# Softmax attention: a joined tile is turned before the preceding tile's value products, and three seams between stages are changed

## What is computed

```python
s = jnp.einsum('bhiqd,bhikd->bhiqk', q_blk, k).astype(jnp.float32) * scale
s = s + bias.transpose(0, 3, 1, 2)[:, :, None]
p = jax.nn.softmax(s, axis=-1)
a = p[:, :, 0] - lam * p[:, :, 1]
return jnp.einsum('bhqk,bhkv->bhqv', a, v.astype(jnp.float32))
...
o_b = rms_norm(o_b.transpose(0, 2, 1, 3), diff_norm_w[i]) * (1 - lambda_init)
...
mixed = jnp.concatenate([o_a, o_b], axis=-1) @ w_out[i]
x = x + g_a[:, None, :] * mixed
```

```python
ya = ya * jax.nn.sigmoid(ya @ glu_w.astype(jnp.float32) + glu_b.astype(jnp.float32))
yb = fnet_mix(ub, f_w)
y = jnp.concatenate([ya, yb], axis=-1).astype(z.dtype) * jax.nn.silu(z)
return y @ w_out
```

## Time and profile before

| | us |
|---|---|
| median of 3 runs (2230.5 to 2232.33) | 2231.55 |
| time of the profiled execution | 2230.68 |
| its span | 2228.9 |
| attention loop, from the first biased map to the last output taken | 393 to 545 |
| block of the product mix begins | 553 |
| block of the product u begins | 1388 |
| block of the product eo begins | 1766 |

### The profile page before, as it was taken

One profiled execution on the slowest core, in us unless ns is written; L12 is line 12 of the kernel. 1 busy time (PEld: TensorE's weight loads), 2 busy tenths in 40 slices (PEclk: granted clock), 3 DMA queues, 4 the chain that ended last, 5 costly groups with the idle time before them and its releaser, 6 DMA issues. The chain is left out here.

```text
span 2228.9 us, 29464 instructions
## 1 busy us (share of the span) xinstructions
PE 2133.6 (96%) x11276; PEld 1735.0 (78%) x11276; DVE 1565.2 (70%) x2299; ACT 812.2 (36%) x1130; POOL 941.4 (42%) x718
## 2 busy tenths in 40 slices
PE   6999999998999999999999999999997999999997
PEld 4887787787777888888777786888877787777876
DVE  5775516998768888888768776869985637764344
ACT  4104433777234333444323224114225323342331
POOL 0222344431425888888556455111000021798710
PEclk9999999999999999999999999999998999999998
DMA  7595733332332333333577764493458323111131
GB/s 276 210 331 167 207 125 115 110 119 76 144 114 84 115 130 131 131 113 103 210 250 265 237 206 171 159 299 120 142 175 304 124 73 119 48 48 49 56 132 76
DMA packets 155430, 337.74 MB, mean 152 GB/s; under 512 B 14038, under 2 KB 92790, under 8 KB 152184
## 3 DMA queue, kind: packets, MB, share of 16 engines
q1 hardware_dynamic: 152292, 330.75, 43.7%
q10 hardware_dynamic: 3000, 5.15, 0.7%
HBM read 259.52 MB, written 93.09 MB: 158 GB/s over the span
## 5 line engine op out<-in xcount | busy, mean ns | idle before, releaser
L282 POOL TENSOR_TENSOR w_lo<-w_staged,w_hi 128x1024 fp32r<-128x1024 f32 x26 | 64.6, 2487 | 355.1 <-ACT w_hi L232 355.0
L2342 POOL TENSOR_TENSOR w_lo<-w_staged,w_hi 128x1024 fp32r<-128x1024 f32 x31 | 80.3, 2591 | 252.3 <-ACT w_hi L2323 252.3
L232 ACT CAST w_hi<-w_staged 128x1024 fp32r<-128x1024 f32 (+1 forms) x33 | 33.8, 1023 | 216.0 <-DMA w_staged<-in_w_u 40.5
L3736 POOL TENSOR_TENSOR w_lo<-w_staged,w_hi 128x512 fp32r<-128x512 f32 x61 | 83.4, 1368 | 59.1 <-ACT w_hi L3732 59.1
L2323 ACT CAST w_hi<-w_staged 128x1024 fp32r<-128x1024 f32 x31 | 32.5, 1049 | 157.9 <-PE ps_in L2351 104.9
L2351 PE MATMUL ps_in<-h_hi,w_hi 128*128 128x512 f32 x272 | 86.9, 400 | 1.0 <-DVE h_lo L1918 1.0
L3732 ACT CAST w_hi<-ff_room 128x512 fp32r<-128x512 f32 x60 | 36.7, 612 | 134.7 <-POOL ff_room L3753 130.2
L2351 PE MATMUL ps_in<-h_lo,w_hi 128*128 128x512 f32 x272 | 85.1, 394 | 0.0
L3440 POOL TENSOR_TENSOR ff_room<-s_par 128x480 f32<-128x480 f32 x32 | 39.6, 1237 | 100.0 <-PE ps_n L3481 50.9
L468 POOL TENSOR_TENSOR w_lo<-w_staged,w_hi 128x512 fp32r<-128x512 f32 x40 | 64.5, 1617 | 22.7 <-ACT w_hi L464 22.5
L3112 PEld LDWEIGHTS ps_attentions<-x_in,att_aT 128*128 128x128 f32 x512 | 59.6, 191 | 13.2 <-issue 10.6
(11 more groups left out here) (822 smaller groups left out, 7026.6 us busy)
## 6 DMA issues: line engine op xcount, KB each, us to landing
w_staged<-in_w_ff SPq DMA_DIRECT2D x46, 512.0 KB, 3.6
x_in<-in_w_ada SPq DMA_DIRECT2D x16, 1024.0 KB, 7.6
scratch_bias<-scratch_line SPq DMA_DIRECT2D x32, 512.0 KB, 7.7
kst_tok<-scratch_bias SPq DMA_DIRECT2D x32, 512.0 KB, 3.3
ada_w<-in_w_ada SPq DMA_DIRECT2D x8, 2048.0 KB, 11.0
scratch_x<-x SPq DMA_DIRECT2D x3, 4096.0 KB, 15.0
scratch_ff_a<-mixed SPq DMA_DIRECT2D x22, 512.0 KB, 2.9
ff_raw<-scratch_ff_a SPq DMA_DIRECT2D x20, 512.0 KB, 4.8
```

Source lines behind the costliest of these rows:

```text
L232: nc.scalar.copy(st.hi[i % 2][:, 0:widths[i]], st.staged[i % 2][:, 0:widths[i]]).then_inc(st.hi_ready, 1)
L282: nc.gpsimd.tensor_tensor(st.lo[i % 2][:, 0:widths[i]], st.staged[i % 2][:, 0:widths[i]], st.hi[i % 2][:, 0:widths[i]].bitcast(F32), ALU.s ...
L2342: nc.gpsimd.tensor_tensor(st.lo[i % 2][:, :], st.staged[i % 2][:, :], st.hi[i % 2][:, :].bitcast(F32), ALU.subtract).then_inc(st.split, 1)
L3736: self.nc.gpsimd.tensor_tensor(self.slot(self.st.lo, q, m), self.weights[m], self.slot(self.st.hi, q, m).bitcast(F32), ALU.subtract).then_ ...
```

## The change

Four things are changed.

1. In the attention loop PE does `turn(n - 1)` before `multiply(n - 2)`, not behind it. DVE's program in the loop stays as it is.
2. The end of the attention: `scale(2)` stands before the last `take`, not behind it; the last head is scaled, turned and placed in two halves of four tiles; and DVE makes only one `f_lo` there, the second one being made at the head of the next block (`low_ready=1`).
3. In `project` the `keep_warm` products are issued before the parts' own waits and not behind them. This changes an order only in the product u (`warm=7`); in the last product, the only other one with `warm`, the parts have nothing to do on PE.
4. In the gate block (`glu`) ACT and DVE split the first two strips of `y` for the product eo already (`split_ahead` and the lines in `mix`), and eo's own `SplitParts` begins at the third strip (`ready=EO_READY`). The tiles `o_hi` and `o_lo` get a place in memory that is free that early.

```diff
@@ both_attentions, PE
             def turn_head(h):
-                pe.wait_ge(scaled, h + 1)
                 if h >= 2:
                     pe.wait_ge(placed, h - 1)
-                for t in range(TT):
-                    last = nc.tensor.transpose(ps_s[:, 2 * (h % 2) + t // 4, t % 4 * P:t % 4 * P + P], o[:, h * TT + t, :], ident)
-                last.then_inc(turned_back, 1)
+                for half in range(2):
+                    if h == HEADS - 1 or half == 0:
+                        pe.wait_ge(scaled, h + half + 1)
+                    for t in range(half * TT // 2, (half + 1) * TT // 2):
+                        last = nc.tensor.transpose(ps_s[:, 2 * (h % 2) + t // 4, t % 4 * P:t % 4 * P + P], o[:, h * TT + t, :], ident)
+                    if h == HEADS - 1 or half == 1:
+                        last.then_inc(turned_back, 1)
...
                     pe.wait_ge(biased, 2 * N)
                     turn_head(0)
+                if 1 <= n <= N:
+                    turn(n - 1)
                 if n >= 2:
                     multiply(n - 2)
-                if 1 <= n <= N:
-                    turn(n - 1)
@@ both_attentions, ACT
-            for h in range(2, HEADS):
+            for h in range(2, HEADS - 1):
                 place(h)
+            for first in range(0, TT, TT // 2):
+                place(HEADS - 1, first, TT // 2)
@@ both_attentions, DVE
                     add_bias(n)
+                if n == N + 2:
+                    scale(2)
                 if n >= 3:
                     take(n - 3)
...
-            scale(2)
             mean(1)
             factor(1)
-            scale(HEADS - 1)
-            for k in range(2):
-                dve.wait_ge(nm.hi_ready, split0 + k + 1)
-                nc.vector.tensor_tensor(f_lo[:, k, :], mixed[:, k, :], f_hi[:, k, :].bitcast(F32), ALU.subtract).then_inc(nm.split, 1)
+            for first in range(0, TT, TT // 2):
+                scale(HEADS - 1, first, TT // 2)
+            dve.wait_ge(nm.hi_ready, split0 + 1)
+            nc.vector.tensor_tensor(f_lo[:, 0, :], mixed[:, 0, :], f_hi[:, 0, :].bitcast(F32), ALU.subtract).then_inc(nm.split, 1)
@@ project, PE
+            keep_warm(nc, st.g, ps[0][:, 0:2 * P], warm)
             for b in before:
                 b.tensor(pe)
-            keep_warm(nc, st.g, ps[0][:, 0:2 * P], warm)
@@ the gate block
             def mix(dve, k):
-                nc.vector.tensor_tensor(y[:, k, :], x[:, k, :], sig[:, k, :], ALU.mult)
+                if k == EO_READY + 1:
+                    dve.wait_ge(tabled, 1)
+                multiplied = nc.vector.tensor_tensor(y[:, k, :], x[:, k, :], sig[:, k, :], ALU.mult)
+                if k == EO_READY + 1:
+                    multiplied.then_inc(tabled, 1)
+                    dve.wait_ge(tabled, 2)
+                    for r in range(EO_READY):
+                        dve.wait_ge(nm.hi_ready, eo_split0 + r + 1)
+                        nc.vector.tensor_tensor(eo_lo[:, r, :], y[:, r, :], eo_hi[:, r, :].bitcast(F32), ALU.subtract).then_inc(nm.split, 1)
...
+                def split_ahead(self, act):
+                    act.wait_ge(gated, EO_READY + 1)
+                    for r in range(EO_READY):
+                        nc.scalar.copy(eo_hi[:, r, :], y[:, r, :]).then_inc(nm.hi_ready, 1)
```

More of the change, by code:

```diff
@@ L261, in _ @@
             for i in range(n, n + 2):
+                if open_gate is not None and i == n:
+                    beside.split_ahead(act)
                 if stats is not None and i == n + 1:
@@ L1554, with __init__ @@
 class SplitParts(Part):
[L1557 removed]
+    def __init__(self, nc, nm, x, kb, hi, lo, open_gate=None, ready=0, low_ready=None):
         self.open_gate, self.ready = open_gate, ready
+        self.low_ready = ready if low_ready is None else low_ready
         self.nc, self.nm, self.x, self.kb, self.hi, self.lo = nc, nm, x, kb, hi, lo
@@ L1567, in scalar @@
             self.nc.scalar.copy(self.hi[:, k, :], self.x[:, k, :]).then_inc(self.nm.hi_ready, 1)
-            if k == 0 and behind_first is not None:
+            if k == self.ready and behind_first is not None:
                 behind_first()
-            if self.open_gate is not None and k == self.open_gate.BEHIND:
+            if self.open_gate is not None and k == self.ready + self.open_gate.BEHIND:
                 self.open_gate.scalar(act)
     def vector(self, dve, behind_first=None):
-        for k in range(self.ready, self.kb):
+        for k in range(self.low_ready, self.kb):
             dve.wait_ge(self.nm.hi_ready, self.split0 + k + 1)
@@ L3240, in factor, with scale @@
                 dve.wait_ge(factored, 5 * q + 5)
-            def scale(h):
-                rows = slice(h * TT, (h + 1) * TT)
+            def scale(h, first=0, tiles=TT):
+                rows = slice(h * TT + first, h * TT + first + tiles)
                 if h == 0 or h == HEADS - 1:
                     dve.wait_ge(taken, rows.stop)
-                nc.vector.tensor_tensor(o[:, rows, :], o[:, rows, :], fac[:, rows].unsqueeze(2).to_broadcast([P, TT, P]),
+                nc.vector.tensor_tensor(o[:, rows, :], o[:, rows, :], fac[:, rows].unsqueeze(2).to_broadcast([P, tiles, P]),
                                         ALU.mult).then_inc(scaled, 1)
@@ L5382, in build @@
         with ExitStack() as ctx:
-            split = SplitParts(nc, nm, mixed, KD, hi, lo, ready=2)
+            split = SplitParts(nc, nm, mixed, KD, hi, lo, ready=2, low_ready=1)
             norm = SplitHalvesKept(nc, g, nm, st, normed, "n2", x, vec("ffn_norm"), mod(SC_F, 0), mod(SH_F, 0), hi, lo, rms, mixed[:, :, :])
@@ L5467, in build @@
         with ExitStack() as ctx:
+            tile(ctx, "edge_of_ya", [P, whole_lines(TT)])
+            eo_at = nc._sbuf_addr_for_side("left")
+            eo_hi, eo_lo = (nc.alloc_sbuf_tensor_at(name, [P, KD, L], F32R, offset=eo_at + 4 * KD * L * i) for i, name in enumerate(("o_hi", "o_lo")))
             ya, sig = tile(ctx, "ya", [P, K5, L]), tile(ctx, "glu", [P, K5, L])
@@ L5532, in build @@
         with ExitStack() as ctx:
+            assert nc._sbuf_addr_for_side("left") == eo_at
+            tile(ctx, "o_room", [P, 2 * KD, L])
+            hi, lo = eo_hi, eo_lo
             work = tile(ctx, "odd_work", [P, 4, L])
-            hi, lo = tile(ctx, "o_hi", [P, KD, L], F32R), tile(ctx, "o_lo", [P, KD, L], F32R)
-            split = SplitParts(nc, nm, y, KD, hi, lo, open_gate=open_even)
+            split = SplitParts(nc, nm, y, KD, hi, lo, open_gate=open_even, ready=EO_READY)
             norm = SplitHalvesKept(nc, g, nm, st, ctx, "n5", x, vec("norm_g", KD, KD), mod(SC_1, 1), mod(SH_1, 1), hi, lo, rms, y[:, :, :])
```

11 lines of the change are left out of this document (6 added, 5 removed).

## The result

The changed kernel takes 2240.56 us (median of 5 runs, 2236.96 to 2245.64), the kernel before 2230.5 us (2228.53 to 2232.33): ratio 1.0042, with 95% interval 1.0026 to 1.0058, so it is 6 to 13 us slower. A later series had it at 2245.33 us against 2233.32 us, 1.0056 (1.0043 to 1.0069). One run each of experiments 5 and 6 took 4298 and 4512 us; the ratios leave them out. The profiled execution took 2236.96 us.

A forecast was written before the change was run, and what follows sets the result against it. DVE's chain bounds the attention, PE fitting around it; PE is busy 96% overall. Attention +14.8, u -2.0, eo -3.9 make +8.9 on 2230.68: 2239.6; with 0.87 for the median, forecast 2240.5 us, range 2236 to 2247.

The forecast's parts named there:

- the second rival: Attention loop: The ring closes at its dear bound, 0.62 us a tile; with full seams +13.1 us, 2244.7 us; chance 0.17.
- The order in the loop: Attention loop: take waits 0.48 us per tile for the value products, 29 times, +13.9 us.
- The ring: Attention loop: join, transposes, value products, take, next join close within one turn; 2.95 us from join to take.
- ring costs less than half: Rival, attention loop: 0.2 us a tile and the seams pay, +0.4 us, 2232 us, no change; chance 0.07.
- the ring doesn't close: Rival, attention loop: products end in time, only the seams are left, -6.4 us, 2225.2 us; chance 0.08.
- Turn 32: Attention, behind the loop: no bias between join and take, so take comes 2.95 us behind the join, not 1.59; +1.36 us.
- The end of the attention: From the last join to mix: scale(2) moved, last head in halves, one f_lo; -0.5 us.
- The fourth rival: Attention loop: PE's waits lower its clock, a tile takes some 8 us, the loop 100 us more; chance 0.01.
- scale(2) and the halves: End of the attention: scale(2) takes 1.86 us beside POOL's casts, mean(1) comes +0.5 us; halves and one f_lo give 1.0.
- The head of mix at nothing: Head of the block after the attention: the second f_lo moved there costs nothing; 1.2 us if its cover were gone.
- u: Head of product u: unused products run in PE's idle time, the third strip is reached earlier; -2.0 us.
- eo: Head of product eo: PE begins 2.3 us earlier, clock stays up, second output strip comes earlier; -3.9 us.

The follow-up runs named there:

- experiment 5: Kernel before with only the changes at u and eo; loop order and end of the attention as before. Ratio 0.9976.
- experiment 6: Changed kernel with the old loop order and scale(2) back behind the last take; last head still in halves. Ratio 0.9962.
- experiment 1: Changed kernel with the loop order of before (value products, then transposes), all other edits kept. Ratio 0.9973.
- experiment 2: Kernel before with only the new loop order (transposes, then value products). Ratio 1.0076.
- experiment 3: Changed kernel with DVE's take put behind the join in turns 3 to 31, PE's new order kept. Ratio 0.9973.
- experiment 9: Changed kernel plus unused products on PE in its last two turns, two before tile 30's transposes and five before tile 31's. Ratio 1.0053.
- experiment 4: Changed kernel with the old order, value products first, in PE's last two turns only. Ratio 1.0029.
- experiment 8: Kernel of experiment 5 without the fourteen records of unused products at the head of u (warm=0). Ratio 0.9966.
- experiment 10: Kernel of experiment 6 plus unused products on PE in the end of the attention (one, three and one). Ratio 0.9964, 2223.19 us.
- experiment 12: The changed kernel itself, unaltered, run again beside the others on one chip. Ratio 1.0056.

## Why the prediction was right, and where its steps were not

The forecast, 2240.5 us, met the first series (2240.56), and the direction and the mechanism hold. That it was met to 0.1 us is luck. By the account of the traces the sum should have been +12.4 and not +8.9. The first series hid these 3.5 us: its difference, +10.1, lies 2.3 under that of the traces, and its median of the kernel before lies 1.05 under the one that the forecast started from. The later series, 2245.33 us, lies nearer to the number of the second rival, 2244.7, though not by its reason. Step by step:

- **The order in the loop: right.** The ring was forecast at 2.95 us and measured 2.98; 0.48 us a tile forecast, (149.04 - 134.30) / 29 = 0.51 measured (from the first to the 31st join), so 14.7 us and not 13.9. (The bound from below was misreckoned: without the transposes' release it is 2.89 - 2.47 = 0.42 a tile and not 0.44.) Experiments 1, 2 and 3 show it from three sides. The "dear ring" and "ring costs less than half" rivals fell with this number, "the ring doesn't close" with the earlier trace rows already and now with experiment 3.
- **Turn 32: right.** +1.36 forecast, 5.76 - 4.38 = +1.38 measured.
- **The end of the attention: wrong.** -0.5 us was forecast from the last join to mix; it was +1.6. The step that failed is that the ring of tile 31 was taken at 2.95 us like any other. It took 4.63, since the clock had fallen; that is 1.7 of the 2.1 us. The fourth rival looked for a falling clock in the steady loop, where PE idles 0.4 us in 4.9 and the clock indeed stays at 1.00 (from 398 to 551 us in the changed kernel); I didn't look at the two turns where there are no scores left and PE's idle time is 2.0 and 2.9 us. In all four traces that have the new order in these turns and nothing to fill them (the changed kernel twice, experiments 2 and 3) the clock fell there. In experiment 9, with the idle time filled, it did not, nor in 4, with the old order: so the idle time is the cause, and the order makes it, though each of these two rests on one trace.
- **scale(2) and the halves: right but for 0.4 us.** 1.86 us beside the casts was forecast for scale(2), about 2.0 measured. Of the +0.5 forecast for mean(1) 0.3 was the ring, so 0.2 the move; it was 0.25 without the ring (experiments 1 and 6) and 0.4 in the changed kernel (mean(1) begins 9.49 us behind the last join against 7.12, of which the late `take` explains 1.96). The halves with one `f_lo` were to give 1.0 and gave 0.75 (experiment 6).
- **The head of mix at nothing: wrong by 0.9.** The second `f_lo` hides as forecast, but the clock is low for 6.8 us there instead of 3.4. This moves by itself (experiment 5), so I can't say how much of the 0.9 belongs to the change.
- **u: -2.0 forecast, -2.27 measured**, by the mechanism named: the third strip sets it (experiment 8).
- **eo: -3.9 forecast, -4.0 measured**, in part by luck: half of 3.68 times 1024/1280 is 1.47 us a strip and not 1.4, by which the second output strip would have come 0.2 us later; measured were 4.20 / 3 = 1.40. PE begins 0.98 us behind the last product and the clock stays up, as forecast from the lack of a counterexample.

What stays open: why the first series lay 2.4 us closer than the second. Both intervals overlap. Stretches at 1.2 GHz that lie at other places and in other number may be the reason (one of 3.4 us costs up to 1.7, an estimate from half the speed); in 28 runs of the kernel before, those with the lower mean clock were the longer ones, by 0.9 us for each 0.001. That they are the reason is not shown.

## What to carry to other kernels

When two engines feed each other, follow from one instruction of the bound engine what its next instruction hangs on, through the new order of the other engine, back to it. If the path closes within one turn, its length is the new pace; here it can be opened on either side, by the old order of PE or by moving one copy of DVE. And treat the first and last turns as stages of their own: they have less work to fill the waits, and idle time of PE there is paid twice, once as a wait and once by the lower clock behind it.

## What the runs showed of the hardware

- An idle gap of PE alone doesn't tell whether its clock falls. Behind 0.98 us at eo it stayed at 1.00; in experiment 10 also behind 1.92 us at mix; behind 2.03 us it stayed in the changed kernel and fell in experiment 2. What repeated was the fall behind two gaps that follow one another: 2.03 and 2.89 us in both traces of the changed kernel, 1.32 and 2.88 us in experiment 3.
- A low clock under a loop that DVE bounds costs little: 6.8 us at 1.2 GHz at the start of the attention loop cost 1.1 us (experiments 4 and 10; in 10 join(5) ends 31.55 instead of 30.48 us behind the first bias), where PE at half speed loses 3.4 (an estimate, half of 6.8). A stretch of 3.4 us there cost nothing: with one the last join but one of the changed kernel ends 156.50 us behind the first bias, without one 156.52 (experiment 12).
- A scale of 128x1024 on DVE takes 1.22 us alone and 1.86 to 2.05 us beside POOL's casts (1.86 in the kernel before, 2053 ns the longest one in the changed kernel).
